# An expert row beside every unit from chunk 40: what moving ten lookups per layer does to a two-layer kernel

## The reference

```python
idx = jnp.take_along_axis(cidx, pos, axis=-1).reshape(PEER_CHUNK, PEER_HEADS * PEER_TOPK)
gate = jax.nn.softmax(top, axis=-1).reshape(PEER_CHUNK, PEER_HEADS * PEER_TOPK)
u_e = jnp.take(u, idx, axis=0)
v_e = jnp.take(v, idx, axis=0)
act = jax.nn.gelu(jnp.einsum('ted,td->te', u_e, xc).astype(jnp.float32))
return jnp.einsum('te,ted->td', (gate * act).astype(v_e.dtype), v_e)
```

## Time and profile before

| | us |
|---|---|
| median of 3 runs | 2063.3 |
| lowest, highest | 2063.12, 2070.76 |
| the profiled execution | 2059.14 |
| its span, first to last instruction | 2057.3 |
| layer 0: first weights / second weights | 260 to 568 / 568 to 883 |
| layer 1: first weights / second weights | 1068 to 1376 / 1376 to 1691 |

### The profile page before, as it was taken

One profiled execution on the slowest core, in us unless ns is written; L12 is line 12 of the kernel. 1 busy time (PEld: TensorE's weight loads), 2 busy tenths in 40 slices (PEclk: granted clock), 3 DMA queues, 4 the chain that ended last, 5 costly groups with the idle time before them and its releaser, 6 DMA issues.

```text
span 2057.3 us, 33110 instructions
## 1 busy us (share of the span) xinstructions
PE 1996.1 (97%) x13084; PEld 1835.8 (89%) x13084; DVE 1376.7 (67%) x2724; ACT 656.1 (32%) x1331; POOL 580.4 (28%) x539
## 2 busy tenths in 40 slices
PE   9999999999999998989999999999999999999999
PEld 9877899899999888977699989999988888777887
DVE  7566589877755545458849977774535637877885
ACT  3455411354400000036541144430000105765554
POOL 1000103767654333200101376754343410000000
PEclk9999999999999999999999999999999999999999
DMA  7536679999999999914468999999999974334565
GB/s 264 195 124 224 246 277 348 372 409 398 381 394 409 409 409 409 380 62 144 155 248 297 374 409 408 398 373 409 409 406 409 409 292 138 113 124 141 189 193 164
DMA packets 169273, 612.42 MB, mean 298 GB/s; under 512 B 19984, under 2 KB 20096, under 8 KB 168864
## 3 DMA queue, kind: packets, MB, share of 16 engines
q1 hardware_dynamic: 107712, 391.63, 51.3%
q0 software_dynamic: 59984, 217.28, 27.2%
q10 hardware_dynamic: 1424, 1.41, 0.2%
HBM read 606.89 MB, written 1.05 MB: 295 GB/s over the span
## 4 chain that ended last, share of the span: by engine, by line
PE 65%; DMA 17%; DVE 14%; ACT 1%; issue 1%; POOL 1%; ACTq 0%; POOLq 0%; DVEq 0%
PE ps L1060 16%; PE ps L1029 15%; DMA plain<-in_peer_v 12%; PE ps L733 5%; PE ps L769 4%; PE ps L772 4%; PE ps L776 4%; PE ps L816 4%; PE ps L736 3%; DVE big L2398 2%; DVE big L2157 2%; PE ps L805 2%; DVE big L2394 2%; PE ps L1016 2%; DMA big<-in_peer_ur,big 1%; PE ps L868 1%
## 5 line engine op out<-in xcount | busy, mean ns | idle before, releaser
L1060 PE MATMUL ps<-big,plain 128*128 128x160 f32 x2576 | 379.6, 307 | 20.0 <-DMA plain<-in_peer_v 17.6
L1060 PEld LDWEIGHTS ps<-big,plain 128*128 128x128 f32 x2576 | 361.9, 194 | 35.6 <-issue 23.3
L2571 DVE SCALAR_TENSOR_TENSOR big<-big 128x1024 f32<-128x1024 f32 x166 | 213.3, 1285 | 216.0 <-DMA big<-in_peer_v,big 214.3
L2151 DVE TENSOR_TENSOR lo<-raw,hi 128x1024 fp32r<-128x1024 f32 (+1 forms) x195 | 236.2, 1219 | 113.2 <-ACT hi L1544 112.5
L3253 POOL DMA_INDIRECT big<-in_peer_v,big x168 | 177.4, 1056 | 289.1 <-PE ps L1060 158.3
L1544 ACT ACTIVATE hi<-raw 128x1024 fp32r<-128x1024 f32 (+1 forms) x195 | 204.8, 1055 | 157.8 <-PE ps L776 53.2
L1029 PE MATMUL ps<-big,plain 128*128 128x160 f32 x1712 | 242.9, 301 | 0.0
L1029 PEld LDWEIGHTS ps<-big,plain 128*128 128x128 f32 x1712 | 234.3, 190 | 0.0
L3253 POOL DMA_INDIRECT big<-in_peer_ur,big x132 | 161.6, 1225 | 149.3 <-DVE big L2565 116.4
L1060 PE MATMUL ps<-big,plain_in_xs 128*128 128x160 f32 x1216 | 174.9, 302 | 5.9 <-DMA plain_in_xs<-in_peer_v 4.9
L2565 DVE CUSTOM_DVE_ANT_0 big<-big 128x1024 f32<-128x1024 f32 x132 | 160.5, 1230 | 26.7 <-DMA big<-in_peer_ur,big 26.6
(11 more groups left out here) (417 smaller groups left out, 2986.9 us busy)
## 6 DMA issues: line engine op xcount, KB each, us to landing
plain<-in_peer_v SPq DMA_DIRECT2D x161, 512.0 KB, 15.6
plain<-in_peer_u SPq DMA_DIRECT2D x107, 512.0 KB, 8.4
plain_in_xs<-in_peer_v SPq DMA_DIRECT2D x76, 512.0 KB, 21.0
plain_in_xs<-in_peer_u SPq DMA_DIRECT2D x68, 512.0 KB, 8.6
big<-in_peer_u SPq DMA_DIRECT2D x64, 512.0 KB, 7.7
raw<-in_ret_vg SPq DMA_DIRECT2D x32, 512.0 KB, 4.2
raw<-in_peer_q SPq DMA_DIRECT2D x24, 512.0 KB, 5.3
raw<-in_ffn_up SPq DMA_DIRECT2D x22, 512.0 KB, 3.5
```

The source lines that it names most:

```text
L1060: ins = e.matmul(us[b // 2].view[:, b % 2 * DENSE:(b % 2 + 1) * DENSE], w[:, b * 128:(b + 1) * 128], experts[:, k, :], start=k == 0 and b ...
L2151: e.tensor_tensor(ul[:, 0:w], raw[:, i % N_RAW, 0:w], uh[:, 0:w].bitcast(F32), ALU.subtract).then_inc(s_lo, 1)
L2571: e.scalar_tensor_tensor(out=sums, in0=rows, scalar=w, in1=sums, op0=ALU.mult, op1=ALU.add).then_inc(s_looked, 1)
```

## The change

From chunk 40 (`EVERY`) on, the schedule puts a look beside both units of each chunk, where it put one beside four units in five. Everything derived from the schedule moves with it: `GATHERS`, `ALL_LOOKED` (15 to 4), `LATER` (143 to 153), `LOOK_UNIT` and with it the gates of the gathers. q = 91 is then the last look of the first weights, and q = 92 to 191 stand beside units 0 to 110 of the second weights. Both layers use the same schedule.

```diff
--- before.py
+++ after.py
@@ -32,7 +32,7 @@
 N_RING = N_FIRST + IN_XS + 1
 N_PLAIN = N_RING + IN_EXPERTS + IN_SUMS
 ROW_SLOTS = [q % 9 if q < 126 else (q - 126) % 6 for q in range(192)]
-YIELDS, GATED, TURNED, LISTED, SPREAD, LOOKS = 15, 14, 22, 23, 26, 8
+YIELDS, GATED, TURNED, LISTED, SPREAD, EVERY, LOOKS = 15, 14, 22, 23, 26, 40, 8
 PAIRS, FOURTHS = 64, 32
 LISTS = PAIRS + FOURTHS
 TWO_PI = 2.0 * math.pi
@@ -244,7 +244,7 @@
             steps[c, j] = list(range(at, min(at + n, GROUPS + 2)))
             at = min(at + n, GROUPS + 2)
             gathers += [q + N_ROWS - (3 if i < 2 else 0) for i in steps[c, j]]
-            n = 1 if c >= LOOKS and q < LISTS and ((2 * (c - LOOKS) + j) % 5 < 4 if c < GATED - 2 or c >= SPREAD else j == 0) else 0
+            n = 1 if c >= LOOKS and q < LISTS and ((2 * (c - LOOKS) + j) % 5 < 4 if c < GATED - 2 or SPREAD <= c < EVERY else c >= EVERY or j == 0) else 0
             looks[c, j] = list(range(q, q + n))
             q += n
         tokens.append(4 * max(0, at - 2))
```

## The result

| | before | after |
|---|---|---|
| median of 12 runs of each on one chip, us | 2064.01 | 2072.47 (2069.24 to 2074.55) |
| ratio after/before, 95% interval | | 1.0039 (1.0030 to 1.0047) |
| profiled execution, span, us | 2057.3 | 2071.6 |

The change costs 0.4%, 8.5 us. The interval of the ratio leaves out 1, so the loss is real, though smaller than the 0.5% that the prediction took for the least a measurement can tell. The time lies 1.5 us above the range given (2053 to 2071), and on the other side of no change than the forecast.

What follows compares the result with a forecast made beforehand. PE was taken to bound the first weights, full DMA the second. Gains of 6.8, 2.6 and 5.9 us less 0.89 us for each of 7.5 units a layer gave 1.9 us faster: median 2061.5 us, range 2053 to 2071.

Steps and rivals of the forecast that it cites:

- Idle DMA recovered: From chunk 40 to 608 us in layer 0, likewise layer 1: added gathers fill idle DMA, 6.8 and 5.9 us gained.
- shift s: End of second weights: units by which the last unit PE waits for comes earlier; 7.5 taken, bounds 5 and 11.
- other loads: Layer 0's second weights: two of the next stage's loads fall behind the full stretch, 2.6 us gained (bounds 1.3 and 2.6).
- What bounds the kernel: PE in the first weights, DMA full at 409 GB/s in the second: 2.45 us of DMA a unit against 2.17 of PE.
- Units no longer under the rows: End of second weights: s units' weights leave the full DMA stretch and are paid at PE's pace, 0.89 us lost each.
- by the gate s is 11: Second weights: the gate for the last gather opens 11 units earlier; with that s the sum is 4.3 us slower.
- The sum: Layer 0 gains 2.7 us, layer 1 loses 0.8: net about 1.9 us faster.
- The signs named: In the changed profile: last look near 839 us, PE's last wait at unit 106 to 109, layer 0's end within 3 us.
- The cover in the first weights: From chunk 40: DVE busy 102 and POOL 97 of 118 us with ten more looks, no PE stall.
- The row queue: Rows land at most one per 2.56 us, so 94 will have landed by 568.3 us, the end of layer 0's first weights.
- The slower one: Chunks 40 to 63: DVE and POOL become the pace, about 24 us slower, 2088; chance 0.09.
- The faster one: Second weights: the last waited-for unit hardly moves (s at most 1), idle DMA still filled, 13.5 us gained, 2050; chance 0.09.

Runs made afterwards that it cites:

- the second profile of before: No edit: the kernel before profiled a second time; median 2062.38 us, span 2060.6 us.
- experiment 4: The change with five looks moved a layer instead of ten (2067.44 us, ratio 1.0019 to before), and with twelve (2072.51 us, ratio 1.0050).
- e1_stretch: The change, with the second weights' looks skipping every sixth unit instead of every eleventh, last look at unit 120: 2059.24 us, ratio 0.9986 to before.
- e2: Before's first weights, but a look beside every unit of the second weights, last look scheduled at unit 110: 2067.56 us, ratio 1.0028 to before.
- e11: The change with two units in eleven skipped, gate three units ahead, layer 0's loads for the next stage later: 2049.73 us, ratio 0.9932 to before.
- experiment 9: Layer 0's next-stage loads later, on the change with looks spread to unit 120, gate four ahead (2053.16 us), or to 121, gate three (2049.73 us).
- e4_more: The change from chunk 34 instead of 40, so twelve looks a layer are moved: 2072.51 us, ratio 1.0050 to before.

## Why the prediction was wrong

The mechanism held: idle DMA is filled in the first weights, and DMA time is left unused behind the last row. What failed are the sizes of three terms of the sum. "Idle DMA recovered" was put at 12.7 us and came to 7.9. The shift s was put at 7.5 units a layer and came to 10.6 and 9.0, 4.1 us more of loss. The other loads were put at 2.6 us and came to 1.3. All three erred to the same side. Against the prediction stand here the second profile of before, and the table; the first of the three sizes, the largest, hangs on that choice of profile.

**What bounds the kernel: right.** In the second weights up to the last look the DMA is the bound (403 to 409 GB/s in every kernel), and PE waits for its weights. In the first weights from chunk 40 it is PE, in after too, where the DMA is full beside it.

**Idle DMA recovered: filled as said, but less of it.** 408 GB/s from 450 us, 409 from 568 to 608. The prediction gave this 12.7 us from the one profile; the second has 3.5 us idle in each layer's first weights, not 5.2 and 4.9, and 1.4 in each second weights. Recovered were 7.0 - 0.6 = 6.4 and 2.8 - 1.3 = 1.5, together 7.9. That term was 4.8 us too large.

**Units no longer under the rows: the mechanism right, and at 0.89 us a unit.** Behind the last look the idle DMA rose by 40.5 - 22.2 = 18.3 us. The units by which the last look came earlier were 116.4 - 105.8 = 10.6 and 118.1 - 109.1 = 9.0; 0.89 x 19.6 = 17.4.

**What s is: here it failed.** 7.5 was taken, 10.6 and 9.0 came: 0.89 x (19.6 - 15) = 4.1 us. The step is the sentence "At PE's pace there, also some 2.5 us a unit, s is between 5 and 7". The time by which the gathers end earlier was estimated at 13 us and up to 4 more; it was 855.6 - 837.4 = 18.2 in layer 0. Turning it into units at 2.5 us each supposes that PE is where it was at any given time. It isn't: every row that lands early takes a unit's weights off the same DMA time, so PE is behind already (the chain leaves it after 25 units, not 45). The same account that gave the loss closes this too: the full stretch is shorter by the s units' weights and by the idle time filled, so 18.2 = 1.28 x s + (3.5 - 0.3) + 1.4, s = 10.6, which is what was counted. In layer 1, with the times counted from chunk 40, it gives 1.28 x 9.0 + 3.3 = 14.8 of 16.7 us, and 1.9 stay unexplained. With the prediction's own upper 17 us and its 6.8 us of idle time, it would have given 8.0, and with the idle time of the second profile 9.7. The bound "by the gate s is 11" was the better value: in after the last gathers wait for PE ("<-PE ps L1060"), and in the kernels in which the gate sets it the last look stands 3 to 4 units behind the gate's unit in layer 0 (113 to 116.4, 102 to 105.8, 112 to 115.4, 116 to 120.0, 118 to 121.1).

The prediction defined s by another mark, the last unit that PE has to wait for, and took the two for one. PE's last wait went from unit 116 to 98 in layer 0 and, but for one of 0.66 us near the end, from 116 to 108 in layer 1: 18 and 8 units. In layer 0 the DMA moved 409 GB/s for another 18.7 us after it, up to the last look. So it is the last look, and not the last wait, at which DMA time begins to lie unused.

**Other loads: half.** Four of the next stage's loads are issued behind the last look of layer 0 in after and three in before, so one changed sides, not two: 1.3 us, the lower bound given, where 2.6 was taken. PE's last wait of layer 0, on its timeline:

```profile
818.75 6.26 PE L1060 MATMUL ps<-big,plain 128*128 128x160 f32 x32 [2.77 <-DMA plain<-in_peer_v]
```

32 records take 4.3 us where nothing holds PE; these two units took 6.26. The window of PE alone shows why (busy, granted clock, DMA share, GB/s):

```profile
818.75:823.00 4.25, 4.25 (x19) 0.60 1.05 414
```

The granted clock was 0.60 there, near the lower of its two levels (1.2 of 2.4 GHz), and 1.00 before and after. In the 18.7 us ahead of it PE had been busy for 12.8 only, waiting for weights. Before's second profile has such dips too (0.53 at 780 to 782 us, 0.50 at 812 to 814), but there PE waits for weights again afterwards (852.12), and the time is lost to the DMA in any case. In after PE waits for nothing from 824 us to the end, so these 1.9 us lengthen the stage. The prediction had no term for the clock.

**The sum.** 4.8 + 4.1 + 1.3 = 10.2 us between the 1.9 faster of the forecast and what the runs gave, 8.5 slower: 10.4. So close an agreement is luck in a table with 2 us of scatter, the more so as counted from the first profile the idle DMA recovered would be 11.3 us and not 7.9. With s = 11 the prediction had 4.3 slower; the idle time and the loads as measured would have made it 19.6 - 7.9 - 1.3 = 10.4 slower, 2 us too much. What made it miss was to lean on the idle time of one execution, and on the queue's time where the account asked for units.

**The signs named.** The last look of layer 0 stood at 837.4 us (839 was said), 252 records stand between 648 and 688 us (fewer than 279), and there is no stall behind chunk 40 in the first weights. Two were missed: PE's last wait, said to be at unit 106 to 109, came at 818.75 in layer 0, with 480 records (30 units) still to go, at unit 98 (in layer 1 it was at 108, but for one of 0.66 us at 1696.14); and layer 0's second weights ended at 888.9 us, 5.5 after before's first profile and 4.8 after the second, where 3 was the limit.

**The cover in the first weights: right.** DVE 99.9 us, POOL 97.3, PE without a stall. POOL's 97 were those of the sum; the up to 12 us more by which DVE's looks might have held it did not come. DVE's idle time fell with the added looks: at L2511, 21.7 us of waits for the gelu became 10.8, in DVE's groups of instructions:

```profile
L2511 DVE SCALAR_TENSOR_TENSOR big<-ps,big 128x384 f32<-128x384 f32 (+24 forms) x27 | 15.6, 578 | 15.1 <-ACT big L1722 10.8 <-issue 4.3
```

The row queue came out nearly as forecast: DVE's timeline at the start of the second weights shows the looks of rows 93 to 95 wait for their rows, so 93 had landed where 94 were forecast.

```profile
572.27 1.23 DVE L2565 CUSTOM_DVE_ANT_0 big<-big 128x1024 f32<-128x1024 f32 x1 [0.59 <-DMA big<-in_peer_ur,big]
574.84 1.23 DVE L2565 CUSTOM_DVE_ANT_0 big<-big 128x1024 f32<-128x1024 f32 x1 [1.33 <-DMA big<-in_peer_ur,big]
577.37 1.22 DVE L2565 CUSTOM_DVE_ANT_0 big<-big 128x1024 f32<-128x1024 f32 x1 [1.30 <-DMA big<-in_peer_ur,big]
...
579.99 0.75 DVE L2569 TENSOR_SCALAR big<-raw,big 128x1024 f32<-128x1024 f32 x1 [0.71 <-DMA raw<-in_peer_v,big]
```

**The rivals.** The slower one did not happen; the time was lost elsewhere, and a first sign of it comes with twelve looks (experiment 4). The faster one is refuted by the unit at the last look, 9 to 11 units earlier, not one; e1_stretch shows what it would have been worth: with 1.0 and 1.8 units of shift the change gains 3 us, not 13, since there were 7.9 us of idle DMA to win, where the rival counted with 12.7 and with 2.6 of other loads. A rival that was not named, that the early gelu or the ten looks in the first weights cost something in themselves, falls with e1_stretch too, which has both.

**What stays open.** The table sets the idle DMA of one execution beside the medians of many. Beside the spans of the same profiles (2060.6 for before) it agrees within 1.6 us in every row, so a part of the 2 us by which it misses e2, after and e11 is scatter between executions: e2's span is 3.3 above before's, where the idle sum has 2.8 and the medians 4.9. After's span is 11.0 us above before's: 8.4 of them lie in the windows of the table, and 2.9 between the end of layer 0's second weights and chunk 40 of layer 1 (381.2 us against 378.3), where both schedules run the same work; there PE's wait for POOL named in experiment 4 was 1.5 us longer. Whether the change had any part in that is not shown. Open too are the rest of the 5.9 us that before with the later gate idles ahead of its last look, of which only layer 0's first 40 us were looked at, and whether loads moved further still (experiment 9) would fill the end.

## What to carry to other kernels

When two streams share a full DMA and one of them runs out first, the rest of the stage is paid at the engine's pace with the DMA half idle: moving work of that stream ahead gains only the idle time it fills, and costs (engine time less DMA time of a unit) for each unit left alone at the end. So spread what remains until the stage's end, with its gate as late as its landing time allows; here that made 8.5 us of loss into 12.5 us of gain with the same bytes. Sum the idle DMA by stretches before and after, from two profiles of the kernel before at least: a term of 13 us read from one was 8 by the other.

## What the runs showed of the hardware

Two busy queues shared the DMA half and half in every kernel: between 600 and 800 us (layer 0) the looks, each waiting for its row, stand 2.56 us apart in the median, twice the 1.28 us of a tile at 409 GB/s. So a gather fetched early is not free even when its slot is: in after the chain left PE after 25 units of the second weights instead of 45. Before's first profiled execution was 4.9 us below the median of its 12 runs (2059.14 against 2064.01); against the second profile 3.7 us of the difference (496.4 - 492.7) lie between the two layers' second weights. The granted clock fell to 0.50 to 0.60 for some 3 us at a time in the second weights of most kernels; in after one such dip, 818.75 to 823, cost 1.9 us, because PE was no longer held by the DMA. POOL's build took 0.79 us at best and 2.96 at worst, with a median of 0.93 to 1.00 us in all kernels but e4_more, where looks stand beside every unit from chunk 34 and it was 1.11; the ten added looks alone moved it little (0.94 and 0.93 in the two profiles of before, 0.95 in after).
